# Halving the moving columns of the inverse products and of the score levels in a two-layer hybrid trunk

## What is computed

```python
# layer 0: HGRN2, chunkwise, 4 heads of 128 (k and q are 128 wide per head)
diff = cum[:, :, :, None, :] - cum[:, :, None, :, :]
decay = jnp.where(mask, jnp.exp(jnp.where(mask, diff, 0.0)), 0.0)
scores = jnp.einsum("bhtd,bhsd,bhtsd->bhts", qc, kc, decay)
# layer 1: RWKV-7, 16 heads of 64, a state that is updated token by token
sa = jnp.einsum("bhvk,bhk->bhv", state, -kkt)
state = (state * wt[:, :, None, :] + sa[..., None] * (kkt * at)[:, :, None, :]
         + vt[..., None] * kt[:, :, None, :])
return state, jnp.einsum("bhvk,bhk->bhv", state, rt)
```

## Time and profile before

| | |
|---|---|
| median of three runs | 4382.2 us |
| span of the profiled execution, which is its own time | 4387.1 us |
| TensorE matmul busy | 3898.0 us (89%) |
| TensorE weight load busy | 2310.2 us (53%) |
| VectorE busy | 1945.6 us (44%) |
| ScalarE busy | 1438.6 us (33%) |
| chain that ended last | TensorE 72%, VectorE 14%, ScalarE 7% |
| L618 and L625, inverse products | 650.1 us of matmul busy, 5120 records |
| L444, products of the score levels | 139.5 us, 1024 records |

### The profile page before, as it was taken

One profiled execution on the slowest core, in us unless ns is written; L12 is line 12 of the kernel. 1 busy time (PEld: TensorE's weight loads), 2 busy tenths in 40 slices (PEclk: granted clock), 3 DMA queues, 4 the chain that ended last, 5 costly groups with the idle time before them and its releaser, 6 DMA issues.

```text
span 4387.1 us, 60627 instructions
## 1 busy us (share of the span) xinstructions
PE 3898.0 (89%) x21962; PEld 2310.2 (53%) x21962; DVE 1945.6 (44%) x4078; ACT 1438.6 (33%) x2603; POOL 138.6 (3%) x151
## 2 busy tenths in 40 slices
PE   2997999999899799999979879999998987999998
PEld 1553565556455356556546536556555644556554
DVE  6355543354245543444315464353342546444352
ACT  1333333233233333333224333233233333233242
POOL 0001000000000100000000010000000001000000
PEclk9999999999999899999999989999999998999999
DMA  7222110101212210110132130110012213100011
GB/s 298 59 88 58 36 30 22 31 30 39 78 49 88 64 40 22 30 31 21 42 95 59 59 83 22 31 30 21 30 56 71 59 59 83 31 28 24 26 34 39
DMA packets 269492, 229.83 MB, mean 52 GB/s; under 512 B 15548, under 2 KB 251256, under 8 KB 266104
## 3 DMA queue, kind: packets, MB, share of 16 engines
q1 hardware_dynamic: 266872, 217.18, 16.0%
q0 software_dynamic: 2304, 8.39, 0.5%
HBM read 208.76 MB, written 16.78 MB: 51 GB/s over the span
## 4 chain that ended last, share of the span: by engine, by line
PE 72%; DVE 14%; ACT 7%; issue 5%; DMA 1%; DVEq 0%; SPq 0%; ACTq 0%
PE bank L545 13%; PE bank L411 12%; PE bank L625 7%; PE bank L618 7%; PE bank L504 6%; PE bank L487 4%; PE bank L614 3%; PE bank L444 3%; PE bank L408 3%; DVE xm L1253 2%; PE bank L651 2%; PE bank L535 2%; PE bank L670 2%; PE bank L664 2%; DMA xm<-in_ada_w 1%
## 5 line engine op out<-in xcount | busy, mean ns | idle before, releaser
L545 PE MATMUL bank<-xm,wring 128*128 128x512 f32 x2048 | 1104.9, 641 | 68.6 <-ACT arena L910 33.8
L411 PE MATMUL bank<-arena,wring 128*128 128x512 f32 x1280 | 580.6, 593 | 14.1 <-ACT xm L756 9.1
L545 PEld LDWEIGHTS bank<-xm,wring 128*128 128x128 f32 x2048 | 341.6, 194 | 322.5 <-issue 207.3
L411 PEld LDWEIGHTS bank<-arena,wring 128*128 128x128 f32 x1280 | 230.8, 190 | 259.6 <-issue 240.6
L618 PE MATMUL bank<-arena 128*128 128x128 f32 x2560 | 338.1, 275 | 0.0
L944 ACT COPY arena<-bank 128x512 f32<-128x512 f32 x320 | 187.3, 585 | 453.8 <-PE bank L614 453.8
L625 PE MATMUL bank<-arena 128*128 128x128 f32 x2560 | 312.0, 275 | 0.0
L618 PEld LDWEIGHTS bank<-arena 128*128 128x128 f32 x2560 | 311.0, 192 | 0.0
L504 PE MATMUL bank<-wring,yT 128*128 128x512 f32 x608 | 275.8, 616 | 32.7 <-DVE yT L1287 22.6
L625 PEld LDWEIGHTS bank<-arena 128*128 128x128 f32 x2560 | 298.7, 192 | 0.0
L950 ACT ACTIVATE arena<-Mcur,arena 128x64 f32<-128x64 f32 x256 | 88.9, 347 | 543.4 <-DVE Mcur L1382 543.4
(11 more groups left out here) (257 smaller groups left out, 5189.5 us busy)
## 6 DMA issues: line engine op xcount, KB each, us to landing
wring<-in_rw_w_rkvz SPq DMA_DIRECT2D x128, 512.0 KB, 3.7
wring<-in_ev_w_in SPq DMA_DIRECT2D x96, 512.0 KB, 5.1
xm<-in_ada_w SPq DMA_DIRECT2D x16, 1536.0 KB, 12.4
wring<-in_ev_w_out SPq DMA_DIRECT2D x32, 512.0 KB, 8.1
wring<-in_rw_w_out SPq DMA_DIRECT2D x32, 512.0 KB, 3.3
xm<-in_x POOLq DMA_DIRECT2D x16, 512.0 KB, 6.2
arena<-in_x SPq DMA_DIRECT2D x16, 512.0 KB, 5.9
residual_scratch<-arena SPq DMA_DIRECT2D x4, 2048.0 KB, 7.6
```

The costliest lines, as they stand in the source:

```text
L411: mm = pe.matmul(pj[:, :], w[:, k, :], hT[:, k, 1:1 + TB], start=(k == 0), stop=(k == KC - 1))
L545: mm = pe.matmul(pj[:, :], w[:, k, :], xmv[MIX_OF[i - 2]][:, k, :], start=(k == 0), stop=(k == KC - 1))
```

## The change

Each product of the inverse levels, and of the score levels n of 1 and more, takes only the 64 later columns as its moving operand, and writes them side by side ("packed") into 64 columns of the bank, 4 products in 256 columns. The stationary operand stays 128 by 128. VectorE then reads the packed 256 columns. `copy_predicated` works on the later columns alone, 256 in place of 512, with the mask cut in the same way. `second_half(t, lv)` becomes `later(t, m)`. Level 0 of the scores and all transposes stay as they are. No instruction is added, removed or moved.

```diff
-        def second_half(t, lv):
-
-            m = 2 << lv
+        def later(t, m):
+
             return t.rearrange("p (c a x m) -> p c a x m", x=2, m=m, a=P // (2 * m))[:, :, :, 1, :]
+
+        def packed(t, m):
+
+            return t.rearrange("p (c a m) -> p c a m", m=m, a=P // (2 * m))
...
-                        mm = pe.matmul(LV[n % 2][:, cc], lhs[:, cc], rhs[:, cc], start=True, stop=True)
+                        if n == 0:
+                            mm = pe.matmul(LV[0][:, cc], lhs[:, cc], rhs[:, cc], start=True, stop=True)
+                        else:
+                            m = HC >> n
+                            mm = pe.matmul(packed(LV[n % 2][:, c * 64:c * 64 + 64], m)[:, 0], lhs[:, cc],
+                                           later(rhs[:, cc], m)[:, 0], start=True, stop=True)
...
-                            mm = pe.matmul(bank[h][:, c * P:(c + 1) * P], r_L[:, cc], r_T[:, cc], start=True, stop=True)
+                            mm = pe.matmul(packed(bank[h][:, c * 64:c * 64 + 64], m)[:, 0], r_L[:, cc],
+                                           later(r_T[:, cc], m)[:, 0], start=True, stop=True)
...
-                            mm = pe.matmul(bank[h][:, c * P:(c + 1) * P], r_TT[:, cc], r_N[:, cc], start=True, stop=True)
+                            mm = pe.matmul(packed(bank[h][:, c * 64:c * 64 + 64], m)[:, 0], r_TT[:, cc],
+                                           later(r_N[:, cc], m)[:, 0], start=True, stop=True)
...
-                        V.copy_predicated(sc, lmask[:, LEVELS - n, None, :].to_broadcast([P, JT, HC]), lv)\
-                            .then_inc(S["h_lvc"], 1)
+                        m = HC >> n
+                        V.copy_predicated(later(h_sc, m), later(lmask[:, LEVELS - n, :], m).to_broadcast([P, JT, HC // (2 * m), m]),
+                                          packed(LV[n % 2][:, 0:JT * 64], m)).then_inc(S["h_lvc"], 1)
...
-                    nc4, tc4 = (second_half(t, lv) for t in (r_N, r_T))
-                    wm = second_half(wmask[:, lv + 1, :], lv).to_broadcast([P, 4, P // (2 * m), m])
+                    nc4, tc4 = (later(t, m) for t in (r_N, r_T))
+                    wm = later(wmask[:, lv + 1, :], m).to_broadcast([P, 4, P // (2 * m), m])
 
                     def half(h):
-                        return second_half(bank[h][:, :], lv)
+                        return packed(bank[h][:, 0:256], m)
```

More of the change, by code:

```diff
@@ L609, in rwkv_prepare @@
                 for lv in range(5):
+                    m = 2 << lv
                     for h in range(2):
```

## The result

The change makes the kernel slower: 4421.25 us (median of four runs, 4421.04 to 4422.52) against 4381.85 us, which is the kernel before with one run more than above. The ratio is 1.0089, with a 95% interval of 1.0075 to 1.0104, so 39 us were lost. The profiled execution has a span of 4419.1 us against 4387.1 us. For the runs, 4432 us was forecast.

The account below looks back on a forecast made before the run. TensorE alone was taken to bound the inverse levels, with weight loads keeping their pace. The terms 0 + 0 - 1.5 - 1.2 + 53 = +50 us on 4382.2 gave 4432 us; 8 in 10 within 4368 to 4456 us.

Parts of the forecast that it names:

- The pace of the inverse products: Inverse levels on TensorE: 5120 records keep stepping at 111 ns, bound by weight loads; 0 us, at best 20 us gained.
- the pace follows the moving columns: Rival, inverse levels: 64 columns step at about 56 ns, a level takes about 3.0 us; 232 us saved, 4150 us, chance 0.05.
- the tails: End of each unit's inverse: the last product's result comes 48 ns earlier, counted once in 32 units; 1.5 us gained.
- The score levels: Score levels n of 1 and more: 896 records step at the same pace as before; 0 us.
- the copies: VectorE's masked copies fall from 731 to about 475 ns, counting only behind a block's last level; 1.2 us gained.
- The clock behind the inverse: First 12 us behind the inverse levels: TensorE's clock falls in 17 more units at 3.1 us each; 53 us lost.
- The clock inside the levels: Rival: the clock falls within the inverse levels, 22.2 us more per unit, 178 us in eight, 710 in all; chance 0.09.
- That nothing happens: Rival: gapless records keep TensorE's clock up behind the inverse, no falls are added; 4379.5 us, chance 0.22.

Follow-up runs that it names:

- probe: The changed kernel plus six bursts of 96 products of constants ahead of the loop over blocks, results unused; 4551.62 us in its one run.
- scores_only: The changed kernel with the inverse products back at full width, score levels and their masked copies still narrow; 4382.6 us, ratio 1.0004.
- inv_only: The changed kernel with the score levels and their masked copies back as before, inverse products still narrow; 4422.79 us, ratio 1.0094.
- thin_fill: The changed kernel plus unused one-column products behind the last inverse level, twelve in a pair's first unit, four in its second; 4455.96 us, ratio 1.0166.
- fill_after: The changed kernel plus unused 512-column products of constants behind the last inverse level, three in a pair's first unit, one in its second; 4352.1 us, ratio 0.9933.
- last_full: The changed kernel with the last of the five inverse levels moving all 128 columns again; 4373.4 us, ratio 0.9978.

## Why the prediction was right, point by point

- **The pace of the inverse products** was forecast not to move, because 128 weight columns take as long to load as 128 moving ones to stream. It holds: 111 ns in the probe and 112 ns in L617 of the changed kernel. The Trainium skill, TensorE: Matmul & The Clock Gate, section LDWEIGHTS (loading the stationary operand), says that loading takes the columns by 1.2 GHz, 107 ns here. The probe comes near that at full clock, with 111 ns a record, but steps at 213 ns once the clock is down. By the table of the Trainium skill, TensorE: Matmul & The Clock Gate, section Back-to-back issue gap, 64 columns would follow at about 60 cycles, for which its row has some 25 ns. No run agrees: the shortest steady step is about 58 ns a record, in the probe, and only where the weights have 64 columns as well. The rival that the pace follows the moving columns is out.
- **The inverse's gain was mis-sized.** "Pace of the inverse products: 0" and 1.5 us for the tails stood for what measured 15.3 us. The step itself did not go to 107 ns. The gain sits at the start of each group of L609, which follows transposes: 0.04 to 0.05 us a group, 0.09 us a level. In the records the second product record of such a group follows the first after 59 ns on average (57 to 64 ns in all 320 groups, 112 before). The prediction's sentence that such a product cannot step faster than 107 ns is wrong there. The term for the tails did not come in at all: a record was to last about 225 ns, but the page has 275 ns for L617 as before and 268 ns for L609, and the pause behind the last of them is as long as it was.
- **The score levels** were forecast at 0 and the copies at 1.2 us; scores_only shows no difference. The copy's length was mis-sized too, 475 ns forecast (450 to 500 as a sign) and 521 ns measured, without effect that scores_only could show:

```profile
L1157 DVE COPY_PREDICATED xm<-lmask,bank 128x256 f32<-128x256 uint8 x112 | 58.4, 521 | 124.6 <-PE bank L433 124.6
```

- **The clock behind the inverse** was the term that decided. The mechanism is right: it falls in 28 units in place of 14, at 0.58 to 0.72 over the 12 us. The size forecast was 17 falls more at 3.1 us, 53 us. Measured are 14 more and 49.7 us in the chains. The prediction missed the last unit of a block, which fell in none of the four blocks, before or after. There the chain's gaps are filled with parts of the output projection (L477), products of 128 rows and 512 columns, from its first chunk on. That this is the reason was not tried, and it does not always hold: in inv_only, with the same inverse, and in the probe one of the four last units falls too, at 0.86. In exchange the falls were somewhat dearer: in the second unit the mean clock is 0.59 and not 0.72, and its chain takes 36.4 us in place of 33.3.
- **The clock inside the levels** does not fall in any of the 32 units, so this rival did not come in. By the Trainium skill, TensorE: Matmul & The Clock Gate, section Part 4: PE-mode transpose, transposes do not count as busy time in the same way. That the levels keep their clock does not prove the opposite; no run removed the transposes.
- **That nothing happens**, as weight loads would count as work, is refuted directly by thin_fill and by the probe's burst of one column.

Both errors of size point the same way: 14 us more gain in the inverse and 3 us less loss in the chains. So the spans differ by 32 us where 50 were forecast. The runs differ by 39 us, which is nearer the forecast partly by luck. The forecast took 4387.1 us as 4.9 us above the median of the runs on both sides, but a span is about 2 us shorter than the run that it belongs to (4419.1 us and 4421.04 us in the changed kernel). The profiled execution of the kernel before was thus some 7 us slower than its median, and that of the changed kernel was not. The 14 falls read from it may be more than the kernel usually has: against the 10 falls of scores_only, 18 were added and 59 us lost in the chains.

## What to carry to other kernels

Before halving the moving side of a float32 product, look at the stationary side: with 128 weight columns, a row of products with 64 moving ones steps at 111 ns a record here, as with 128. Then ask what the thinner stream does to TensorE's clock at the next pause: here a kernel that was bound by 128-column loads and streams alike lost 50 us in stretches that the change does not touch, while TensorE's busy share stayed at 89%. Read the granted clock of the stretches behind a pause, unit by unit; where it falls, a full-width product of constants in the time that is idle anyway, or full width in the last few products ahead of it, bought it back here (4352.1 us in fill_after, 4373.4 us in last_full, from 4421.25).

## What the runs showed of the hardware that was not expected

- Unused products in TensorE's idle time make the kernel faster. With a single one, none of the 16 second units of the pairs falls, neither on top of the change (12 fell) nor in the kernel before (5 fell).
- A thin record following full ones costs less than its load: the step of 59 ns at the start of each L609 group. The probe shows it too, 58 ns at the start of the burst of 64 columns (L368) behind the one of 128. Why the load is partly hidden there and not later was not tried.
- The kernel before varies more from run to run (4377.27 to 4389.5 us in 13 runs) than the changed one (4421.04 to 4422.52 in four). That fits falls that happen in some of its units by a narrow margin, and in the changed kernel in nearly all; but the profile shows one execution of each, so this stays an argument.
